# Chunked recurrence of an RWKV block: b and k side by side, u and v on opposite row halves, 128-wide matmuls

## The chip, the cores and the metric

The kernel runs on one core of one Trainium2 chip. The metric is device time in microseconds (us), the median of the runs shown. The engines are TensorE (PE for its matmuls, PEld for its weight loads), VectorE (DVE), ScalarE (ACT), GpSimd (POOL) and SyncE (SP), which issues most DMAs.

## The reference

The program computes a transformer block with attention and a state-space branch, and then a second block. The second block's core is a recurrence that runs in two directions over 256 context tokens and then 1024 tokens, for 8 heads of 64 channels. The change touches this recurrence alone.

```python
def wkv_scan(s0, r, w, k, v, a, b, reverse):
    def step(s, inp):
        r_t, w_t, k_t, v_t, a_t, b_t = inp
        sa = jnp.einsum('bhvk,bhk->bhv', s, a_t)
        s = s * w_t[:, :, None, :] + sa[..., :, None] * b_t[:, :, None, :] + v_t[..., :, None] * k_t[:, :, None, :]
        return s, jnp.einsum('bhvk,bhk->bhv', s, r_t)
    ...
    y, s = lax.scan(step, s0, xs, reverse=reverse)

    # in rwkv_bidir, for each direction d:
    kd = k * (1 + (a - 1) * k_a_h)
    y, s = wkv_scan(s0, r, decay, kd, v, -kk, kk * a, rev)
    y_sum = y_sum + y
```

## The kernel before

`rwkv_chunks` (L2125) does the recurrence in 20 chunks of 64 tokens (`NCK` = 20, `CK` = 64). The first four (`CTX_CK`) are context and give no output; the other 16 do. Both directions d = 0 and 1 run at once, with buffers of their own. A buffer has 128 partitions, two heads of 64 channels one above the other, and `HP` = 4 such pairs behind each other.

For one chunk the steps are these.

- POOL scales the inputs by the decays: `b_raw`, `b_scaled` (L2225, L2232) make b in `bst`; `k_gain`, `k_bias`, `k_raw`, `k_scaled` (L2240 to L2262) make k in `kst`; `a_scaled` and `r_scaled` (L2270, L2280) fill the two halves of `ar`. `v_staged` (L2287) copies v, and `state` (L2295) makes the next state `S` from `sum`. `k_gain` needs the chunk's rates and decays, `ac`, which SP loads two chunks ahead (L2204), once `b_scaled`, `k_scaled` and `r_scaled` of the chunk two before are done.
- PE multiplies b with a and r (`lower`, L2611) and k with a and r (`keys`, L2672). DVE cuts them to triangles with masks in `T.minus` and `T.plus`, into `lm` and `lk` (L2482, L2488), one operation of 512 elements per direction and product.
- A triangular matrix is inverted in levels. Level l is `chained_x` on PE (L2622), `factored` on ACT (L2373), `turned_x`, a transpose, on PE (L2632), `transposed` on ACT (L2378), `advanced` on PE (L2645) and a predicated copy on DVE (L2494). DVE's `first` (L2476) starts it, and `inverted` on PE (L2652) and `inverse` on DVE (L2500) end it.
- With the inverse come the right-hand side, `right_side` and `right_side_of_state` (L2658, L2666), the solution u (`solved`, L2679), the outputs (L2687, L2693) and the next state (L2727). `b_rows`, `k_rows` and `v_rows` (L2698, L2708, L2716) are transposes of b, k and v that `state` and the outputs take.

In `rc_x<-...` and the like, `rc_` is the phase's prefix. Matmuls of 64 rows by 64 columns use one quadrant of the array: `chain`, `crossing` and `staying` (L2575, L2583, L2593) place them. A float32 matmul stands in the trace as two records on PE and two on PEld, a transpose as one on each.

The order of the work is written out by hand. Each engine has one loop over k (POOL L2308, ACT L2406, DVE L2543, PE L2736) in which steps of chunks k - 1, k - 2 and so on are interleaved, and each engine takes its queue strictly in that order. Waits are on semaphores by count. Two of them matter here: POOL's `b_raw` of chunk c waits for the transposes of b of chunk c - 2,

```python
pool.wait_ge(joint["brows_done"], c - 1)
```

and `k_raw` of chunk c for those of k of chunk c - 2 (`rows_done`) and for `keys` (`pk_done`). In POOL's loop `b_raw(k - 1)` stands ahead of the rest of chunk k - 2's scaling:

```python
b_raw(k - 1, 1)
b_raw(k - 1, 0)
k_scaled(k - 2, 1)
...
a_scaled(k - 2, 1)
k_raw(k - 1, 0)
k_gain(k, 0)
k_gain(k, 1)
state(k - 4, 0)
state(k - 4, 1)
```

## Time and profile before

| | |
|---|---|
| runs before | 2673.08, 2678.0, 2678.87 us; median 2678.0 |
| span of the profiled execution | 2672.4 us, 54306 instructions |
| PE busy | 2315.8 us (87%) |
| DVE busy | 1610.5 us (60%) |
| ACT busy | 1047.9 us (39%) |
| POOL busy | 658.7 us (25%) |
| the recurrence's stretch | about 1385 to 1854 us from the span's start |
| DVE `first` of direction 1 starts, chunks 2 and 5 | 1437.65 and 1499.53 us |
| the same, chunks 6 and 18 | 1521.20 and 1798.65 us |

The profiled execution's span of 2672.4 us lies 5.6 us under the median of the runs and 0.7 us under the fastest of them. The shares of busy time are averages over many phases. What bounds the recurrence is read from its own stretch: from the timeline of each engine there, from the waits, and from what ended each of them. "issue" as the releaser of an idle time means that the engine waited for nothing that the profile shows.

### The profile page before, as it was taken

Reading aid. Unit: us, or ns where it says so; the run is one execution under the profiler, and the core shown is the slowest. Engines: PE = TensorE matmul, PEld = TensorE weight load, DVE = VectorE, ACT = ScalarE, POOL = GpSimd, SP = SyncE. Lnnn points to the kernel's source line nnn. Section 1 sums busy time; section 2 is a strip of 40 time slices with the busy share of each in tenths; the row PEclk is TensorE's granted clock in tenths of the full one; section 3 lists DMA queues with packets and bytes.
Section 4 is the critical chain, followed back from the end, with each engine's and each line's share of the span. In section 5 each row is a group of like instructions: output and inputs, shape, how many; then the busy total and the mean of one; then the engine's idle time right before and its main releaser. Section 6 shows DMA issues by size and latency. Waiting matters only on the chain. (4 is left out here: it accounts for less than half of the span.)

```text
span 2672.4 us, 54306 instructions
## 1 busy us (share of the span) xinstructions
PE 2315.8 (87%) x23052; PEld 1827.8 (68%) x23052; DVE 1610.5 (60%) x1961; ACT 1047.9 (39%) x1745; POOL 658.7 (25%) x659
## 2 busy tenths in 40 slices
PE   4998988799989479999758888888983999999993
PEld 2876755468868368888527777776671788888883
DVE  5991659531124555566474444443657999999994
ACT  3112541321022510000345555554231777777773
POOL 0321568113310023222025655551000100000000
PEclk7999999999999689999669999998995999999997
DMA  5232014511122345111161111102232999999994
GB/s 223 99 123 73 1 50 138 157 54 48 52 86 95 108 164 195 63 36 32 44 221 27 28 28 28 28 20 77 96 145 102 376 408 404 397 398 393 396 381 163
DMA packets 135636, 397.84 MB, mean 149 GB/s; under 512 B 56218, under 2 KB 67994, under 8 KB 107890
## 3 DMA queue, kind: packets, MB, share of 16 engines
q1 hardware_dynamic: 124468, 360.02, 36.2%
q0 software_dynamic: 4608, 16.78, 2.6%
q10 hardware_dynamic: 6336, 17.80, 1.8%
q8 instruction: 172, 2.82, 0.4%
q14 instruction: 52, 0.43, 0.1%
HBM read 341.05 MB, written 53.50 MB: 148 GB/s over the span
## 5 line engine op out<-in xcount | busy, mean ns | idle before, releaser
L3871 DVE TENSOR_TENSOR ex_wl<-ew_raw,ex_wh 128x2048 fp32r<-128x2048 f32 x192 | 435.7, 2290 | 41.5 <-ACT ex_wh L3833 38.1
L3833 ACT ACTIVATE ex_wh<-ew_raw 128x2048 fp32r<-128x2048 f32 x192 | 367.7, 1919 | 109.6 <-PE ex_U L3777 40.0
L130 PE MATMUL sp_acc<-b2h_hi,sp_wh 128*128 128x512 f32 (+1 forms) x528 | 195.2, 370 | 14.5 <-POOL sp_wl L1731 14.5
L130 PE MATMUL sp_acc<-b2h_lo,sp_wh 128*128 128x512 f32 (+1 forms) x528 | 195.0, 369 | 0.0
L130 PE MATMUL sp_acc<-b2h_hi,sp_wl 128*128 128x512 f32 (+1 forms) x528 | 194.6, 369 | 0.0
L2494 DVE COPY_PREDICATED rc_x<-b_level,rc_chain 128x256 f32<-128x256 uint32 x160 | 64.5, 445 | 166.2 <-PE rc_chain L2580 165.7
L3754 POOL DMA_INDIRECT x<-ex_o,ex_at x16 | 26.5, 1656 | 494.6 <-DVE ex_o L3894 494.6
L1729 POOL CAST sp_wh<-sp_w 128x1024 fp32r<-128x1024 f32 x26 | 29.1, 1120 | 407.1 <-DMA sp_w<-in_w_conv 230.1
L130 PEld LDWEIGHTS sp_acc<-b2h_hi,sp_wh 128*128 128x128 f32 x528 | 100.3, 190 | 32.3 <-POOL sp_wl L1731 14.9
L2580 PE MATMUL rc_chain<-rc_x,rc_lm 64*64 64x64 f32 x3200 | 94.2, 227 | 20.9 <-issue 14.8
L130 PEld LDWEIGHTS sp_acc<-b2h_hi,sp_wl 128*128 128x128 f32 x528 | 100.3, 190 | 16.5
L130 PEld LDWEIGHTS sp_acc<-b2h_lo,sp_wh 128*128 128x128 f32 x528 | 100.3, 190 | 16.4
L2373 ACT ACTIVATE rc_t<-rc_chain 128x256 f32<-128x256 f32 x200 | 73.7, 387 | 92.6 <-PE rc_chain L2580 90.4
L130 PE MATMUL merge_acc<-merge_hh,merge_wh 128*128 128x512 f32 x256 | 102.9, 402 | 7.7 <-POOL merge_wl L1035 7.2
L130 PE MATMUL pr_acc<-h_hi,pr_wh 128*128 128x512 f32 x224 | 89.5, 399 | 15.9 <-POOL pr_wl L210 14.2
L3775 PE MATMUL ex_G<-ex_wh,ex_xh 128*128 128x512 f32 x256 | 102.0, 398 | 1.4 <-DVE ex_xl L3876 1.4
L130 PE MATMUL merge_acc<-merge_hh,merge_wl 128*128 128x512 f32 x256 | 102.1, 399 | 0.0
L130 PE MATMUL merge_acc<-merge_hl,merge_wh 128*128 128x512 f32 x256 | 101.9, 398 | 0.0
L3775 PE MATMUL ex_O<-ex_wh,ex_hh 128*128 128x512 f32 x256 | 99.8, 390 | 1.6 <-DVE ex_hl L3887 1.6
L3775 PE MATMUL ex_U<-ex_wh,ex_xh 128*128 128x512 f32 x256 | 101.0, 394 | 0.0
L3777 PE MATMUL ex_G<-ex_wh,ex_xl 128*128 128x512 f32 x256 | 100.5, 393 | 0.0
L3776 PE MATMUL ex_G<-ex_wl,ex_xh 128*128 128x512 f32 x256 | 100.1, 391 | 0.0
(522 smaller groups left out, 5983.8 us busy)
## 6 DMA issues: line engine op xcount, KB each, us to landing
ew_raw<-in_exp_gate SPq DMA_DIRECT2D x64, 1024.0 KB, 8.2
ew_raw<-in_exp_up SPq DMA_DIRECT2D x64, 1024.0 KB, 9.3
ew_raw<-in_exp_down SPq DMA_DIRECT2D x64, 1024.0 KB, 7.8
b2p_pT<-in_ada_w SPq DMA_DIRECT2D x32, 512.0 KB, 6.0
rc_ac<-ac SPq DMA_DIRECT2D x40, 256.0 KB, 4.0
b_pj<-in_ada_w SPq DMA_DIRECT2D x8, 1024.0 KB, 12.3
ssm_wm<-in_w_merge SPq DMA_DIRECT2D x16, 512.0 KB, 3.5
ac<-rp_ac SPq DMA_DIRECT2D x4, 2048.0 KB, 7.1
```

Source lines behind the costliest of these rows:

```text
L130: ins = nc.tensor.matmul(out, w[a][:, k, :], h[b][:, k, cols], start=(first and n == 0), stop=(last and n == 2))
L1729: nc.gpsimd.tensor_copy(wh[:, i % 2], w[:]).then_inc(q["w_rounded"], 1)
L2373: A.activation(paired(t[d]["t1"][:]), chained(d), ACT.Copy, scale=-1.0).then_inc(q[d]["t1_ready"], 1)
L2494: V.copy_predicated(paired(b["x"][:, c % 2]), over(T.level[d][l + 1][:].bitcast(u32)), chained(d)).then_inc(s["x_next"], 1)
L2580: last = M(X[d][c * CK:(c + 1) * CK, f, at:at + w], l[k, h], r[k, h], start=True, stop=True)
L3754: nc.gpsimd.indirect_dma_start(x2, bass.IndirectOffsetOnAxis(at[:, x:x + 1], 0), o[:, x % 2, :], None, compute_op=ALU.add).then_inc(scatte ...
L3775: nc.tensor.matmul(acc[:, c], ah[:, k, :], wh[:, s, kk, c], start=(k == 0), stop=False)
L3776: nc.tensor.matmul(acc[:, c], ah[:, k, :], wl[:, s, kk, c], start=False, stop=False)
L3777: last = nc.tensor.matmul(acc[:, c], al[:, k, :], wh[:, s, kk, c], start=False, stop=(k == KD - 1))
L3833: nc.scalar.activation(wh[:, n % RING], raw[:, n % RING], ACT.Copy).then_inc(q["w_hi"], 1)
L3871: V.tensor_tensor(wl[:, n % RING], raw[:, n % RING], wh[:, n % RING].bitcast(f32), ALU.subtract).then_inc(q["w_lo"], 1)
```

## The change

b and k of a head pair now lie side by side in one buffer `bk`, with the two halves swapped between even and odd pairs of heads (`key_slots`). `lower` is one set of matmuls with 128 stationary columns (b and k) and 128 moving ones (a and r), out in `near`; `keys` is gone. The first product, which `first` reads, is made apart by `firsts`, in `crossing`'s bank. `masked` on DVE takes the place of `lower` and `keys` there, two operations of 512 elements per direction. u and v lie in opposite row halves of `uv`, so the outputs and the state are matmuls over all 128 rows (`stacked`) instead of two accumulated ones over 64. The minus signs on u and on the rows of b move into the masks. To fill `uv` ACT evicts u and v by halves of the partitions, four operations each per chunk instead of two. The transposes of b and k come by pairs of heads (`key_rows(c, 0)` where `b_rows` stood, `key_rows(c, 1)` where `k_rows` stood), each with b and k of two pairs, and both `b_raw` and `k_raw` wait for both.

```diff
@@ POOL
                         if c >= 2:
-                            pool.wait_ge(joint["brows_done"], c - 1)
-                        G.tensor_tensor(b["bst"][:, c % 2], nkk[:, :, at(c, d):at(c, d) + CK], b["ac"][:, c % 2, 0], ALU.mult).then_inc(s["b_raw"], 1)
+                            pool.wait_ge(joint["rows_done"], 2 * (c - 1))
+                        G.tensor_tensor(key_slots(d, c)[0], halves(nkk[:, :, at(c, d):at(c, d) + CK]), halves(b["ac"][:, c % 2, 0]), ALU.mult).then_inc(s["b_raw"], 1)
...
                         if c >= 2:
-                            pool.wait_ge(joint["pk_done"], c - 1)
-                            pool.wait_ge(joint["rows_done"], c - 1)
+                            pool.wait_ge(joint["rows_done"], 2 * (c - 1))
@@ ACT
-                    solved(k - 2, 0)
-                    solved(k - 2, 1)
+                    solved(k - 2, 0, 0)
+                    solved(k - 2, 0, 1)
+                    solved(k - 2, 1, 0)
+                    solved(k - 2, 1, 1)
@@ DVE
                     first(k - 1, 1)
-                    lower(k - 1, 1)
-                    lower(k - 1, 0)
                     first(k - 1, 0)
+                    masked(k - 1, 1)
+                    masked(k - 1, 0)
...
-                    keys(k - 1, 1)
-                    keys(k - 1, 0)
@@ PE
+                def stacked(l):
+
+                    for j, e, d, f in product(range(HP // 2), range(2), range(2), range(2)):
+                        at = (2 * d + j) * CK
+                        last = M(W[f * CK:(f + 1) * CK, e, at:at + CK], *l(t[d], f, j, e), start=True, stop=True)
                     return last
...
+                def firsts(c):
+                    if runs(c):
+                        each("b_scaled", c + 1)
+                        each("a_scaled", c + 1)
...
                 def lower(c, d):
                     if runs(c):
                         b, s, sl = t[d], q[d], c % 2
                         pe.wait_ge(s["b_scaled"], c + 1)
+                        pe.wait_ge(s["k_scaled"], c + 1)
...
-                        chain(d, 0, CK, b["ar"][:, sl, :, 0:CK], b["bst"][:, sl])
-                        chain(d, 2 * CK, 2 * CK, b["bst"][:, sl], b["ar"][:, sl]).then_inc(s["low_done"], 1)
+                            pe.wait_ge(s["near_ready"], 2 * c)
+                        for h, f in product(range(HP), range(2)):
+                            k = slice(f * CK, (f + 1) * CK)
+                            last = M(near(d)[:, f, :, h], b["bk"][k, sl, h].rearrange("p a t -> p (a t)"), b["ar"][k, sl, h].rearrange("p (o t) -> p o t", o=2), start=True, stop=True)
+                        last.then_inc(s["low_done"], 1)
...
                 for k in range(NCK + 2):
                     chained_x(k - 2, 0, 4)
                     turned_x(k - 2, 4)
+                    firsts(k - 1)
                     lower(k - 1, 1)
+                    lower(k - 1, 0)
                     right_side(k - 2)
-                    lower(k - 1, 0)
                     inverted(k - 2)
                     chained_x(k - 1, 1, 0)
                     right_side_of_state(k - 2)
                     chained_x(k - 1, 0, 0)
                     turned_x(k - 1, 0)
-                    keys(k - 1)
...
-                    b_rows(k - 1)
+                    key_rows(k - 1, 0)
...
-                    k_rows(k - 1)
+                    key_rows(k - 1, 1)
```

On POOL no row changes its place. In one pass of the loop, from `b_raw` to `a_scaled`, the program before has these rows. A semaphore can stand under the name of one whose number it took over: `n1_inverted` is the one for the transposes of b, `n1_w_loaded7` that of `keys`, `n1_normed` the one for the transposes of k.

```order
L2225 TENSOR_TENSOR rc_bst<-b2k_nkk,rc_ac 128x256 [waits n1_inverted,rc_loaded10]
L2225 TENSOR_TENSOR rc_bst<-b2k_nkk,rc_ac 128x256 [waits n1_inverted,rc_loaded00]
L2262 TENSOR_TENSOR rc_kst<-rc_kst,rc_e_neg 128x256 [waits rc_decays1,rc_k_raw1]
L2280 TENSOR_TENSOR rc_ar<-b2p_pT,rc_e 128x4x64 [waits n1_w_loaded7,rc_decays1]
L2280 TENSOR_TENSOR rc_ar<-b2p_pT,rc_e 128x4x64 [waits n1_w_loaded7,n1_scaled]
L2255 TENSOR_TENSOR rc_kst<-rc_tmp,b2p_pT 128x256 [waits n1_normed,n1_w_loaded7,rc_k_bias1]
L2232 TENSOR_TENSOR rc_bst<-rc_bst,rc_e_neg 128x256 [waits n1_scaled,rc_b_raw0]
L2262 TENSOR_TENSOR rc_kst<-rc_kst,rc_e_neg 128x256 [waits n1_scaled,rc_k_raw0]
L2246 TENSOR_TENSOR rc_tmp<-rc_tmp,rc_ka 128x256 [waits rc_k_gain0]
L2270 TENSOR_TENSOR rc_ar<-b2k_nkk,rc_e 128x4x64 [waits n1_c_ready,rc_decays1]
```

The changed program has the same ten there; `n1_inverted` is now `rows_done`.

```order
L2242 TENSOR_TENSOR rc_bk<-b2k_nkk,rc_ac 128x2x2x64 [waits n1_inverted,rc_loaded10]
L2242 TENSOR_TENSOR rc_bk<-b2k_nkk,rc_ac 128x2x2x64 [waits n1_inverted,rc_loaded00]
L2280 TENSOR_TENSOR rc_bk<-rc_bk,rc_e_neg 128x2x128 [waits rc_decays1,rc_k_raw1]
L2298 TENSOR_TENSOR rc_ar<-b2p_pT,rc_e 128x4x64 [waits rc_low_done1,rc_decays1]
L2298 TENSOR_TENSOR rc_ar<-b2p_pT,rc_e 128x4x64 [waits n1_lo_done,n1_transposed]
L2272 TENSOR_TENSOR rc_bk<-rc_tmp,b2p_pT 128x2x128 [waits n1_inverted,rc_k_bias1]
L2250 TENSOR_TENSOR rc_bk<-rc_bk,rc_e_neg 128x2x2x64 [waits n1_transposed,rc_b_raw0]
L2280 TENSOR_TENSOR rc_bk<-rc_bk,rc_e_neg 128x2x128 [waits n1_transposed,rc_k_raw0]
L2264 TENSOR_TENSOR rc_tmp<-rc_tmp,rc_ka 128x256 [waits rc_k_gain0]
L2288 TENSOR_TENSOR rc_ar<-b2k_nkk,rc_e 128x4x64 [waits n1_c_ready,rc_decays1]
```

Nothing moved in the queue, but the first row and the sixth now wait for one and the same semaphore.

On PE, from the last transposes of chunk k - 2 to the first `advanced` of chunk k - 1, the program before has these rows.

```order
L2604 MATMUL rc_turned<-all_ident,rc_x 128x128 x4
L2580 MATMUL rc_chain<-rc_bst,rc_ar 64x64 x8
L2580 MATMUL rc_chain<-rc_ar,rc_bst 64x128 x8
L2590 MATMUL rc_crossing<-rc_v,rc_lk 64x64 x16
L2580 MATMUL rc_chain<-rc_bst,rc_ar 64x64 x8
L2580 MATMUL rc_chain<-rc_ar,rc_bst 64x128 x8
L2597 MATMUL rc_turned<-rc_xt,rc_t 64x64 x16
L2580 MATMUL rc_chain<-rc_x,rc_lm 64x64 x8
L2597 MATMUL rc_own_half<-rc_S,rc_ar 64x64 x16
L2580 MATMUL rc_chain<-rc_x,rc_lm 64x64 x8
L2604 MATMUL rc_turned<-all_ident,rc_x 128x128 x4
L2590 MATMUL rc_crossing<-rc_ar,rc_kst 64x128 x16
```

The changed program has these.

```order
L2631 MATMUL rc_turned<-all_ident,rc_x 128x128 x4
L2610 MATMUL rc_crossing<-rc_bk,rc_ar 64x64 x16
L2658 MATMUL rc_chain<-rc_ar,rc_bk 128x2x64 x16
L2610 MATMUL rc_crossing<-rc_uv,rc_near 64x64 x16
L2624 MATMUL rc_turned<-rc_xt,rc_t 64x64 x16
L2602 MATMUL rc_chain<-rc_x,rc_near 64x64 x8
L2624 MATMUL rc_own_half<-rc_S,rc_ar 64x64 x16
L2602 MATMUL rc_chain<-rc_x,rc_near 64x64 x8
L2631 MATMUL rc_turned<-all_ident,rc_x 128x128 x4
```

The products of b and k come together ahead of `right_side`, and the 16 matmuls of `keys` between the transposes and `advanced` are gone. Later in the pass the outputs and the state are each one row of 16 matmuls in place of eight rows of 4.

## Rows read from the trace of the kernel before

**Rows 1.** Page, TensorE's granted clock in 40 slices, tenths of full speed.

```profile
PEclk7999999999999689999669999998995999999997
```

**Rows 2.** Windows, three context and twelve output chunks: us, busy (records) by engine.

```profile
1437.65:1499.53 61.88, 54.62 (x1829) 45.88 (x1823) 28.21 (x63) 34.81 (x114) 38.55 (x61) 1.00 0.14 31
1521.20:1798.65 277.45, 236.51 (x8454) 205.07 (x8446) 120.61 (x289) 140.28 (x458) 150.73 (x243) 1.00 0.11 26
```

**Rows 3.** DMA queues, same two stretches (output chunks first): packets, MB, share.

```profile
q8 instruction: 68, 1.11, 1.7%
```

```profile
q8 instruction: 15, 0.25, 1.7%
```

**Rows 4.** Waits of PE: who waited for whom, us in total, times, longest.

```profile
PE rc_chain L2580 <- issue: 28.4, 37, 1.6
```

**Rows 5.** Timeline of PE, an output chunk: start, length, records, [idle before].

```profile
1662.72 1.15 PE L2597 MATMUL rc_own_half<-rc_S,rc_ar 64*64 64x64 f32 x32
...
1665.66 1.10 PE L2590 MATMUL rc_crossing<-rc_ar,rc_kst 64*64 64x128 f32 x32
1666.59 0.64 PE L2580 MATMUL rc_chain<-rc_t,rc_xt 64*64 64x64 f32 x32
...
1674.81 0.66 PE L2604 MATMUL rc_own_half<-all_ident,rc_kst 128*128 128x128 f32 x4
...
1676.91 0.45 PE L2580 MATMUL rc_chain<-rc_x,rc_lm 64*64 64x64 f32 x12 [0.94 <-issue]
...
1682.38 0.46 PE L2580 MATMUL rc_chain<-rc_bst,rc_ar 64*64 64x64 f32 x16
```

**Rows 6.** Timeline of POOL, the same chunk, and two rows of the one before.

```profile
1654.61 0.73 POOL L2262 TENSOR_TENSOR rc_kst<-rc_kst,rc_e_neg 128x256 f32<-128x256 f32 x1
...
1661.44 1.18 POOL L2295 TENSOR_TENSOR rc_S<-rc_sum,rc_e_end 128x256 f32<-128x256 f32 x2
```

```profile
1670.45 1.42 POOL L2225 TENSOR_TENSOR rc_bst<-b2k_nkk,rc_ac 128x256 f32<-128x256 f32 x2 [5.26 <-PE rc_own_half L2604]
...
1672.52 1.32 POOL L2280 TENSOR_TENSOR rc_ar<-b2p_pT,rc_e 128x256 f32<-128x256 f32 x2
1675.63 0.72 POOL L2255 TENSOR_TENSOR rc_kst<-rc_tmp,b2p_pT 128x256 f32<-128x256 f32 x1 [1.79 <-PE rc_own_half L2604]
...
1676.99 0.73 POOL L2262 TENSOR_TENSOR rc_kst<-rc_kst,rc_e_neg 128x256 f32<-128x256 f32 x1
...
1678.25 0.69 POOL L2270 TENSOR_TENSOR rc_ar<-b2k_nkk,rc_e 128x256 f32<-128x256 f32 x1
...
1682.57 0.61 POOL L2240 TENSOR_TENSOR rc_tmp<-rc_ac,rc_ka 128x256 f32<-128x256 f32 x1 [0.24 <-DMA rc_ac<-ac]
1683.14 1.18 POOL L2295 TENSOR_TENSOR rc_S<-rc_sum,rc_e_end 128x256 f32<-128x256 f32 x2
```

**Rows 7.** Timeline of PE, a context chunk: first `advanced`, and `k_rows`.

```profile
1464.02 0.63 PE L2580 MATMUL rc_chain<-rc_t,rc_xt 64*64 64x64 f32 x28
...
1471.15 0.66 PE L2604 MATMUL rc_own_half<-all_ident,rc_kst 128*128 128x128 f32 x4
```

**Rows 8.** Timeline of ACT: the evictions of u in the chunk of rows 5.

```profile
1671.76 0.66 ACT L2388 ACTIVATE rc_u<-rc_crossing 128x256 f32<-128x256 f32 x2 [0.46 <-PE rc_crossing L2590]
```

**Rows 9.** Timeline of PE in an earlier phase, other tile shapes (rows*columns of the array).

```profile
440.45 3.71 PE L896 MATMUL s_pZ<-s_um,s_v 128*64 128x128 f32 x64 [0.48 <-issue]
444.10 3.70 PE L874 MATMUL s_pF<-b_pj 128*128 128x512 f32 x8
```

```profile
458.75 1.16 PE L914 MATMUL s_pB<-s_ca,s_x 64*128 64x128 f32 x16
459.84 0.71 PE L909 MATMUL s_pB<-s_wi,s_um 128*128 128x128 f32 x4
```

**Rows 10.** Windows of PE near chunk 19: us, busy (records), granted clock.

```profile
1819.20:1822.80 3.60, 2.01 (x88) 1.00 0.00 0
1822.80:1826.20 3.40, 3.40 (x84) 0.50 0.02 5
```

201 lines of the change are left out of this document (106 added, 95 removed).

## The prediction, as it stood before the changed kernel ran

> **What bounds the kernel now.** I read the granted clock and the busy shares by slice first [rows 1], then the recurrence alone, for nothing outside it changes. From one start of `first` to the next a chunk with outputs takes 23.1 us (277.45 / 12) and a context chunk 20.6 us (61.88 / 3) [rows 2]. PE is busy 85% of both stretches at full clock; DVE, ACT and POOL are at 43 to 62%.
>
> The next view is what PE's idle time ends on, and most of it is "issue": 28.4 us in 37 waits at one line alone [rows 4]. These gaps stand in the middle of a group of matmuls, as the 0.94 us ahead of the last 12 records of a `chained_x` [rows 5], so no semaphore explains them. The DMA view gives the clue: 68 instruction fetches in the output stretch, one every 4.08 us, and 15 in the context stretch, one every 4.13 us [rows 3]. PE and PEld have 16900 and 3652 records there [rows 2], so 248 and 243 to a fetch, and 16.4 and 16.9 ns to a record. Two stretches with different work thus run at one rate per instruction. I take it that **PE is bound by the fetching of its own code**, at about 16 ns a record, with dependences close behind.
>
> The last view is POOL beside PE, because POOL makes what each chunk starts from. Call S the start of `lower`, A the first `advanced`, K the end of `k_rows`. In the chunk shown K is 1675.47 and the next S 1682.38 [rows 5]. POOL's last operation that `lower` needs ended at 1678.94 [rows 6], 3.4 us early. After S it is `state` that counts: `right_side_of_state` starts at 1662.72, and POOL's states ended at 1662.62 [rows 5, 6]. So that wait is on the edge already, and A follows it.
>
> **The change part by part.** *Fewer PE instructions.* Per chunk `keys` and `lower` have 48 matmuls now and `firsts` and `lower` 32 then; the state goes from 32 to 16, the outputs from 32 to 16. A matmul is four records. That is 192 records less in an output chunk and 128 in a context chunk. At 16.4 ns they would be worth 3.1 and 2.1 us, if fetching stayed the bound. The array's own work hardly falls, because all four quadrants are in use now too: `keys` takes 0.93 us for 16 matmuls of 128 columns [rows 5].
>
> *`b_raw` waits for more.* It waited for the transposes of b, at 1670.45; now it waits for all of `key_rows`, the place of `k_rows`, where `k_raw` waits today, at 1675.63 [rows 6]. Queued behind it on POOL are `k_scaled`, `r_scaled` twice, `k_raw`, `b_scaled`, `k_scaled`, `k_bias` and `a_scaled`, and PE's `firsts` waits for the last. From `b_raw` to the end of `r_scaled` is 3.39 us (1673.84 less 1670.45), from `k_raw` to the end of `a_scaled` 3.31 us (1678.94 less 1675.63), and `k_raw` starts 0.16 us after K. So S comes 0.16 + 3.39 + 3.31 + 0.1 = 6.96 us after K; PE's own work in between fills at most the 6.91 us of this chunk, fetch gap of 0.94 us included. What is late next is `state`. POOL has it behind `k_gain`, which waits for a DMA that is issued once `k_scaled` is done. From the end of `k_scaled` to the end of both states it takes 6.60 us (1684.32 less 1677.72) and in the chunk before 7.28 us (1662.62 less 1655.34) [rows 6]; I take 6.9. Hence K to states is 0.16 + 3.39 + 2.09 (1675.63 to 1677.72) + 6.9 = 12.55 us.
>
> *From there to A.* `right_side_of_state`, `chained_x` and the transposes take some 1.8 us on PE and ACT's copy after them 0.5: an estimate of 2.4 us with a semaphore's delay, where rows 5 show 3.87 us with `keys` (0.93) and one fetch gap (0.7) in it. K to A is then 12.55 + 0.1 + 2.4 = **15.05 us**. The 4.0 us of PE work between S and `right_side_of_state` (`firsts`, both `lower`, `right_side`, `inverted`) and the DVE masks lie beside POOL's states and cost nothing; they end some 1.6 us before the states do.
>
> *From A to K.* In the output chunk it is 8.88 us (1666.59 to 1675.47) [rows 5], about 9.6 in the mean of the period, and in the context chunk 7.79 us [rows 7]. In the output chunk 64 records go, 1.0 us, and waits ahead of A leave fetches time to run ahead: 8.2 us. ACT has two evictions of u more in front of the level-2 `factored`, 0.27 us each by start to start (0.66 less 0.39) [rows 8]; in an output chunk the outputs on PE cover them, in a context chunk they add up to 0.5 us, against 0.4 of fetch gaps gone: 7.9 us. The four evictions of v and the 64-partition shape I price alike; nothing waits on them while POOL is late.
>
> *New shapes.* The outputs become 32 records over 128 rows and 64 columns of the array. 64 such records with 128 moving columns took 3.65 us, 57 ns each, and 16 of the 64-row shape 1.09 us, 68 ns each [rows 9]; half the columns give 0.9 us if the load keeps up and 1.8 us if it doesn't. Now they take 0.95 us. I take 1.1, near the lower end, since the quadrant matmuls keep up already. That makes A to K **8.4 us** with outputs. POOL's strided outputs into `bk` no row shows; below zero is excluded, equal is my value, as `ar` is strided already, and 10% more would be 0.7 us a chunk. The masks are four DVE operations of 512 elements before and after.
>
> The Trainium skill, "TensorEngine Tiling (Array Packing)", Key Properties, says that changing the tiling mode drains TensorE. The trace agrees as far as it goes: in rows 9 the short group costs 0.18 us more than its records at the pace of the long one. The change adds about five such changes of mode to a chunk, two of them between A and K; the rest lie where PE waits. By this rule alone A to K would be 0.35 us longer than the columns give, by the row's 1.1 us it is 0.15.
>
> *The sum.* An output chunk: 15.05 + 8.4 = 23.45 against 23.1 us, +0.35 over 13 chunks: +4.5. A context chunk: 15.05 + 7.9 = 22.95 against 20.6, +2.35 over 3: +7. The first period has no state to wait for: +1.5. The last one with transposes has no `k_gain` ahead of the state: -1.2. After it POOL gates nothing and PE's shorter code counts: -2. Together +9.8 us.
>
> *The clock.* PE will stand idle about 2.5 us ahead of `firsts` and 1.6 us ahead of `right_side_of_state`. After a stretch with 1.6 us idle of 3.6 us the granted clock was 0.50 for the next 3.4 us, the lower of its two levels, 1.2 GHz [rows 10]. Work in such a stretch takes double, so up to 1.7 us late; mostly it falls into the slack ahead of the states. I add 0.3 us for each of 17 chunks: +5. On the span of 2672.4 us this gives 2687, and on the median of 2678.0 about **2693 us**.
>
> **The rivals.** *Fetching stays the bound* and POOL keeps up. Every chunk then gains: 14 x 3.1 + 5 x 2.1 = 54 us, so 2624 us. For it speaks the even rate of records; against it that POOL's queue is strict and its 6.7 us after K stand in the rows. It needs POOL to do the ten operations in under 5 us. Chance 0.05.
>
> *POOL gates, but A to K shrinks to what the dependences ask*, 7.4 us, since the fetches are always ahead. An output chunk is then 22.45 us, -0.65 x 13 = -8.5; with the rest, and no loss by the clock, 2678 - 8.5 + 5.3 = 2675 us. It decides from an A to K under about 7.6 us. Chance 0.17, split between faster and same.
>
> *The new shapes and the clock cost more*: 1.8 us for the outputs (+0.7 x 14 = 10) and a half-speed stretch on the path in each chunk (+1.2 more x 17 = 20): 2723 us. It decides if the low clock lasts beyond `right_side_of_state`. Chance 0.13.
>
> *The change does not take away what it says*: the records per chunk stay. The program's order shows them gone, so I give it nothing.
>
> **How the numbers follow.** My forecast has 0.65, from 2680 to 2708 (A to K and the DMA off by 0.5 us each, over 17 chunks). A measurement of this kernel tells about 0.2% (5.4 us) from no change. Faster by more: the first rival and half of the second, 0.13. Same: the rest of the second and a little of the forecast's low end, 0.15. Slower: 0.72. The range 2669 to 2722 leaves out the first rival, and the ends of the others.
>
> **What would show it.** Right: `b_raw` starts 0.2 us after `key_rows(c, 1)`, `firsts` starts 6.9 to 7.1 us after it on `a_scaled`'s release, K to A is 15 us; context chunks 22 to 23.5 us; fetches 4.6 us apart, few gaps inside groups; dips of the granted clock between 1400 and 1830. Wrong: `firsts` without a wait, context chunks at 18.5 us, or A to K under 7.6 us with outputs.

## The result, and the profile of the changed kernel

The changed kernel took 2720.0 us (median of 4 runs, 2715.6 to 2725.2) against 2676.7 us for the kernel before (4 runs, 2673.1 to 2678.9). The ratio is 1.016, with a 95% interval from 1.014 to 1.017: slower by 43 us. I had forecast 2693 us, slower by 15. The direction and the gate on POOL were right, the size was not. The profiled execution of the changed kernel, 2716.7 us, had a mean granted clock of 0.925 and the other three 0.921 to 0.923, so the profile shows a little less half clock than the median run has.

All but a little of it is in the recurrence. It ended 36.9 us later after the start of the span (1890.2 against 1853.3 us). The span grew by 42.5 us, from 2672.4 to 2714.9. The other 5.6 us lie in the phases behind the recurrence, which the change does not touch. Over the kernels of this study that stretch took from 816 to 828 us in no order that I can relate to the edits, so I give it no cause. Below, K is the end of the last key rows of a chunk (of the k rows in the kernel before), S the start of `firsts` (of `lower` there) and A the first `advanced`; a period goes from one K to the next.

The page of the changed kernel first: TensorE's granted clock in 40 slices, to be laid beside rows 1, and the queue of instruction fetches (packets, MB, share of 16 engines), 159 where the page of before has 172.

```profile
PEclk8999999899999599999769899999995899999996
...
q8 instruction: 159, 2.61, 0.4%
```

The windows view gives the two kinds of chunk: start and end, length, then busy time and records of PE, PEld, DVE, ACT and POOL, granted clock, DMA share, GB/s. The first line is twelve chunks with outputs, from one first `advanced` to another, the second three context chunks, both of the changed kernel. The third is the same twelve output chunks of the kernel before.

```profile
1526.41:1820.06 293.65, 245.72 (x7297) 214.54 (x7297) 122.51 (x290) 162.85 (x505) 149.55 (x240) 0.96 0.11 25
1438.37:1508.40 70.03, 55.58 (x1596) 47.43 (x1596) 26.27 (x59) 40.02 (x125) 37.60 (x60) 0.95 0.11 26
```

```profile
1505.62:1782.75 277.13, 236.32 (x8457) 204.93 (x8452) 122.17 (x290) 140.28 (x457) 150.34 (x240) 1.00 0.12 27
```

An output chunk takes 24.5 us instead of 23.1, though PE executes 193 records less in it (7297 + 7297 over twelve chunks against 8457 + 8452). And the clock is no longer 1.00.

What ends PE's idle time has changed altogether. Where rows 4 had "issue" in the middle of groups, the waits of PE in the twelve output chunks (waiting line, its releaser, us in total, times, longest) now read:

```profile
PE rc_crossing L2610 <- POOL rc_ar L2288: 27.6, 12, 3.4
PE rc_chain L2602 <- ACT rc_xt L2396: 7.5, 13, 0.7
PE rc_crossing L2617 <- ACT rc_uv L2408: 6.3, 11, 0.6
PE rc_chain L2602 <- issue: 4.2, 5, 1.2
```

L2610 is `firsts`: once per chunk it waits 2.3 us for POOL's `a_scaled`. The "issue" gaps have almost gone. The third line is one that I had argued away: the outputs wait for ACT's evictions of u.

The chain from POOL to PE stands in the timelines of one chunk. PE (start, length, tile rows*columns, records, idle time before and its releaser): the outputs and the last key rows, then `firsts`, `lower`, `right_side` and `right_side_of_state`.

```profile
1585.45 1.15 PE L2617 MATMUL rc_crossing<-rc_near,rc_uv 128*64 128x64 f32 x32 [0.59 <-ACT rc_uv L2408]
...
1587.16 0.66 PE L2740 MATMUL rc_own_half<-all_ident,rc_bk 128*128 128x128 f32 x4
...
1594.98 0.69 PE L2610 MATMUL rc_crossing<-rc_bk,rc_ar 64*64 64x64 f32 x32 [2.45 <-POOL rc_ar L2288]
1595.61 2.06 PE L2658 MATMUL rc_chain<-rc_ar,rc_bk 64*128 64x128 f32 x32
1597.60 0.69 PE L2610 MATMUL rc_crossing<-rc_uv,rc_near 64*64 64x64 f32 x32
...
1599.74 1.09 PE L2624 MATMUL rc_own_half<-rc_S,rc_ar 64*64 64x64 f32 x30 [0.30 <-issue]
```

POOL in the same chunk: `b_raw`, `r_scaled`, `a_scaled`, the states.

```profile
1587.96 1.42 POOL L2242 TENSOR_TENSOR rc_bk<-b2k_nkk,rc_ac 128x256 f32<-128x256 f32 x2 [9.97 <-PE rc_own_half L2740]
...
1590.04 1.33 POOL L2298 TENSOR_TENSOR rc_ar<-b2p_pT,rc_e 128x256 f32<-128x256 f32 x2
...
1593.96 0.67 POOL L2288 TENSOR_TENSOR rc_ar<-b2k_nkk,rc_e 128x256 f32<-128x256 f32 x1
...
1598.45 1.18 POOL L2313 TENSOR_TENSOR rc_S<-rc_sum,rc_e_end 128x256 f32<-128x256 f32 x2
```

The key rows end at 1587.82 (1587.16 + 0.66), `b_raw` starts 0.14 us later after 9.97 us of waiting, `a_scaled` ends at 1594.63, and `firsts` starts at 1594.98: K to S is 7.16 us. The states end at 1599.63 and `right_side_of_state` follows 0.11 us behind. That is the chain as forecast.

The new thing is the clock. Here is the same stretch of PE in a chunk five further on:

```profile
1714.10 1.13 PE L2610 MATMUL rc_crossing<-rc_bk,rc_ar 64*64 64x64 f32 x32 [2.44 <-POOL rc_ar L2288]
1715.16 3.78 PE L2658 MATMUL rc_chain<-rc_ar,rc_bk 64*128 64x128 f32 x32
1718.87 1.13 PE L2610 MATMUL rc_crossing<-rc_uv,rc_near 64*64 64x64 f32 x32
...
1721.17 1.04 PE L2624 MATMUL rc_own_half<-rc_S,rc_ar 64*64 64x64 f32 x30
```

And the windows of PE over 6.80 us from `firsts` on, in this chunk and in the undisturbed one (length, busy with records, granted clock):

```profile
1714.10:1720.90 6.80, 6.80 (x134) 0.55 0.36 81
...
1594.90:1601.70 6.80, 6.42 (x196) 1.00 0.35 79
```

The same `lower` takes 3.78 us instead of 2.06. With the clock at 0.50 (1.2 GHz) `right_side_of_state` starts 7.07 us after `firsts` instead of 4.76: the work that was to lie beside POOL's states outlasts them by 2.3 us. Of the 18 periods between key rows, nine contain such a stretch of half clock, 3.4 or 6.8 us long, and in each it sets in within 1.3 us of the start of `firsts`, while PE stands idle there or just after. All five periods in which PE is idle for 3.2 us or more between K and S have one; of the other 13, with 2.1 to 2.5 us, four have. The kernel before has none in its output chunks.

### The profile page after: what moved, and what is told of

Same layout as the page of the kernel before. It is cut to its first block and busy times, and to the rows that moved or that the text cites. A ratio compares the mean times of both kernels' runs of the same rounds, so it can differ in the third digit from the quotient of the medians.

```text
span 2714.9 us, 50905 instructions
## 1 busy us (share of the span) xinstructions
PE 2335.3 (86%) x21292; PEld 1847.0 (68%) x21292; DVE 1611.3 (59%) x1961; ACT 1085.5 (40%) x1825; POOL 660.7 (24%) x659
## 5 line engine op out<-in xcount | busy, mean ns | idle before, releaser
L3803 PE MATMUL ex_O<-ex_wh,ex_hl 128*128 128x512 f32 x256 | 100.7, 393 | 0.0
L3802 PE MATMUL ex_O<-ex_wl,ex_hh 128*128 128x512 f32 x256 | 100.7, 393 | 0.0
```

Source lines behind the costliest of these rows:

```text
L3802: nc.tensor.matmul(acc[:, c], ah[:, k, :], wl[:, s, kk, c], start=False, stop=False)
L3803: last = nc.tensor.matmul(acc[:, c], al[:, k, :], wh[:, s, kk, c], start=False, stop=(k == KD - 1))
```

## Experiments

Times are medians with the ratio to the kernel before in the same rounds; "half clock" is its mean time per output chunk in the profiled execution. Chunk lengths are means of 13 output chunks from K to K. The kernel before took 2671.7 to 2676.7 us in the rounds of the several runs, so a difference of a few us between runs of different rounds says nothing.

| kernel | us | ratio (95%) | output chunk, us | K to S | S to `right_side_of_state` | A to K | half clock |
|---|---|---|---|---|---|---|---|
| before | 2676.7 | 1 | 23.11 | 5.78 | 4.65 | 9.50 | 0 |
| changed | 2720.0 | 1.016 (1.014 to 1.017) | 24.52 | 7.36 | 5.49 | 9.14 | 2.1 |
| e2_late_wait | 2715.6 | 1.015 (1.012 to 1.018) | 25.37 | 7.12 | 5.58 | 9.23 | 2.6 |
| e3_filled_wait | 2706.9 | 1.013 (1.010 to 1.015) | 24.49 | 7.55 | 5.09 | 9.32 | 0.3 |
| e4_split | 2709.5 | 1.013 (1.011 to 1.016) | 24.95 | 5.83 | 5.21 | 10.14 | 0.3 |
| e5_order | 2650.4 | 0.992 (0.989 to 0.994) | 20.92 | 4.80 | 4.37 | 9.08 | 0 |
| e5b_order | 2651.6 | 0.989 (0.987 to 0.991) | 20.87 | 4.81 | 4.34 | 9.09 | 0 |
| e6_before_order | 2671.9 | 0.999 (0.998 to 1.000) | 23.09 | 5.71 | 4.24 | 9.85 | 0.3 |
| e7_order_u | 2641.7 | 0.987 (0.984 to 0.989) | 20.63 | 4.93 | 4.31 | 8.77 | 0 |
| e7b_order_u | 2635.1 | 0.986 (0.984 to 0.988) | 20.57 | 4.93 | 4.29 | 8.70 | 0.3 |
| e8_after_u | 2712.2 | 1.012 (1.010 to 1.014) | 24.55 | 7.37 | 6.12 | 8.56 | 3.9 |
| e9_order_u_split | 2668.0 | 0.999 (0.998 to 1.000) | 22.12 | 4.89 | 6.11 | 8.64 | 0 |
| e10_after_split | 2815.0 | 1.055 (1.051 to 1.058) | 29.94 | 7.37 | 10.41 | 8.94 | 11.6 |
| e11_split_filled | 2727.3 | 1.020 (1.018 to 1.023) | 25.07 | 7.17 | 6.34 | 9.06 | 0.5 |

A 0.3 in the last column is a single stretch of 3.4 us in 13 chunks. In e3, e4, e6 and e7b it sets in 2.6 to 19 us after S, away from the wait ahead of `firsts`. So a rare stretch occurs without that wait too; what the experiments below are about is its coming in half of the periods or more.

### The wait alone (e2_late_wait)

One line of the change, put into the kernel before:

```diff
                         if c >= 2:
-                            pool.wait_ge(joint["brows_done"], c - 1)
+                            pool.wait_ge(joint["rows_done"], c - 1)
```

> The kernel before with one edit: b_raw of chunk c waits for rows_done (c-1), the transposes of the k rows, where it waited for brows_done. Nothing else of the change is in it; PE's 1,792 records per output chunk and the u and v evictions stay. Theory (the gate and what it does to the clock): from the end of k_rows to the start of the next lower 7.1 to 7.2 us instead of 5.8 (7.2 in the profile of the changed kernel), so an output chunk of about 24.4 us instead of 23.1, context chunks about 23 instead of 20.0, which is 13 x 1.3 + 3 x 2.6 = 25 us before the clock; and the longer idle time of PE brings stretches of half clock into the chunks, as in the changed kernel, with 5 to 15 us more. 2,700 to 2,720 us. Rival (PE goes on being limited by the fetches of its own instructions, the wait is taken up by them): under 5 us more than the kernel before, 2,677 to 2,682. Second rival (the half clock comes from the new 128-wide shapes): +20 to +27 us and no half clock between 1,440 us and 1,830 us of the span.

Measured: 2715.6 us. This one wait, with no other part of the change, makes the kernel as slow as the whole change does. The timeline of PE shows the end of the k rows and the next `lower`, 1603.59 to 1610.50:

```profile
1602.93 0.66 PE L2604 MATMUL rc_own_half<-all_ident,rc_kst 128*128 128x128 f32 x4
...
1610.50 0.46 PE L2580 MATMUL rc_chain<-rc_bst,rc_ar 64*64 64x64 f32 x16 [1.27 <-issue]
```

```profile
1517.19:1821.15 303.96, 246.46 (x8457) 215.36 (x8453) 122.03 (x290) 139.72 (x457) 149.83 (x240) 0.95 0.11 25
```

K to S is 6.91 us and the clock 0.95, with the old shapes. So the half clock does not need the 128-wide matmuls, and the fetches of PE's instructions do not hide the wait. Both rivals fall. The chunk is even longer than the changed kernel's (25.4 against 24.5 us; I expected 24.4). The difference lies between `right_side_of_state` and A, 3.45 us against 2.52, where the 16 matmuls of `keys` still stand.

The half clock does not always set in at the same place as in the changed kernel. Of the nine output chunks that have it, three have it from within 1.1 us of S; in the other six it sets in 3.9 to 6.0 us after S, in or within 0.9 us behind a second gap of 1.8 to 2.9 us. That gap is the wait for POOL's states in one case and "issue" in five, where it ends 1.4 to 1.6 us after the end of an instruction fetch. So one later wait brings the half clock, but in this kernel mostly together with a gap of the fetches, and the run does not part the two. The expectation counts 1,792 records in a chunk; the profile has 1409, and 1216 in the changed kernel. The difference of 192 or 193 is the same.

### Work in the wait (e3_filled_wait)

In the changed kernel, five matmuls into a bank that `firsts` overwrites, ahead of its waits:

```diff
                 def firsts(c):
                     if runs(c):
-                        each("b_scaled", c + 1)
-                        each("a_scaled", c + 1)
                         if c >= 2:
                             each("summed", c - 1)
+                            for _ in range(5):
+                                M(W[:, 0, 0:256], T.ident[:], T.masks[0][:].rearrange("p a t -> p (a t)"), start=True, stop=True)
+                        each("b_scaled", c + 1)
+                        each("a_scaled", c + 1)
```

> The changed kernel with five matmuls of 256 columns more per chunk on PE (their result is overwritten and never read), placed where PE waits for POOL's b_scaled and a_scaled ahead of firsts; about 2.1 us of work inside a wait of 3 us or more. Theory (the stretches of half clock follow from PE's idle time at that wait): the stretches inside the output chunks, 2.1 us of half clock per chunk on average, go or become rare, the time from the start of firsts to right_side_of_state falls from 5.5 to 4.7 us, and an output chunk takes 23.6 us instead of 24.5: 13 to 20 us less than the changed kernel, about 2,703. Rival (the half clock follows from what PE does in the rest of the chunk, the 128-column keys gone and 64-row work in their place): the stretches stay, time within 3 us of the changed kernel or above it.

Measured: 2706.9 us, 13 us less than the changed kernel with more work in it. The timeline shows the filler in the place of the idle time, and `lower` at its full speed behind it; the windows view has the clock at 0.99 over twelve output chunks.

```profile
1634.00 2.32 PE L2643 MATMUL rc_crossing<-b_masks,all_ident 128*128 128x256 f32 x10
1636.25 0.72 PE L2610 MATMUL rc_crossing<-rc_bk,rc_ar 64*64 64x64 f32 x32
1636.90 2.06 PE L2660 MATMUL rc_chain<-rc_ar,rc_bk 64*128 64x128 f32 x32
```

```profile
1520.11:1813.99 293.88, 265.37 (x7416) 229.03 (x7417) 121.89 (x290) 162.82 (x505) 149.44 (x240) 0.99 0.11 25
```

Half clock fell from 2.1 to 0.3 us per chunk. The chunk itself did not reach the 23.6 us that I expected: the filler takes 2.3 us and starts only when PE gets to it, so `firsts` came late in half of the chunks (K to S up to 8.2 us). That the stretches follow from what PE does in this wait is shown, and the gain is mostly spent on the filler. Whether the filler helps because it ends the idle time or because it is dense work, this run cannot tell. e5_order below has neither the wait nor a filler, and no half clock in its output chunks.

### More records (e4_split)

In the kernel before, each 128-column matmul of `lower` and `keys` as two of 64 columns:

```diff
-                        last = M(X[d][c * CK:(c + 1) * CK, f, at:at + w], l[k, h], r[k, h], start=True, stop=True)
+                        for o in range(0, w, CK):
+                            last = M(X[d][c * CK:(c + 1) * CK, f, at + o:at + o + CK], l[k, h], r[k, h, o:o + CK], start=True, stop=True)
```

> The kernel before with each matmul of 128 columns in lower and keys issued as two of 64 columns: the same products and columns, 32 matmuls and with them 128 records more per chunk (64 matmuls x 2 records). Nothing of the waits changes. Theory (PE is limited by the fetch of its own records, 16.4 to 16.9 ns each): 128 x 16.4 to 16.9 ns = 2.1 to 2.2 us per chunk, 18 chunks, +35 to +40 us where nothing hides it: about 2,713. Rival (the pauses in the middle of the groups are not the price of a record; the chunk is set by POOL or by the round of dependent steps): the 32 matmuls go into waits, 2,677 to 2,690 us.

Measured: 2709.5 us, 35 us more. The windows view and the instruction queue over twelve output chunks:

```profile
1514.76:1813.40 298.64, 246.55 (x9228) 214.28 (x9224) 121.99 (x290) 140.41 (x456) 150.41 (x240) 0.99 0.11 25
```

```profile
q8 instruction: 74, 1.21, 1.7%
```

A fetch comes every 4.04 us (298.64 / 74), with 9% more records than in the kernel before, where it was 4.08. The chunk grew by 1.84 us, the context chunk by 2.07, against 2.1 forecast from 16.4 ns a record. Not all of it need be fetching: the split groups also take longer on PE itself, `keys` 1.36 us against 1.10 and each 128-column part of `lower` 0.75 against 0.62, some 0.5 us in a chunk.

The traces have a more direct sign. In the twelve output chunks of the kernel before PE has 39 "issue" gaps of more than 0.4 us, 36 us in all, and each of them ends 1.26 to 1.55 us after the end of a fetch in queue q8. Between the gaps PE takes up 32 matmul records and 32 loads in about 0.6 us, about 10 ns each, far faster than the mean of 16.4 ns. So it is the arrival of the code that it waits for, not a fixed pace of issuing.

### POOL's order (e5_order, e5b_order, e6_before_order)

The changed kernel with `b_raw` and `k_raw` behind everything that `firsts` and `lower` need:

```diff
                     a_scaled(k - 2, 0)
-                    b_raw(k - 1, 1)
-                    b_raw(k - 1, 0)
                     k_scaled(k - 2, 1)
                     r_scaled(k - 2, 1)
                     r_scaled(k - 2, 0)
-                    k_raw(k - 1, 1)
                     b_scaled(k - 2, 0)
                     k_scaled(k - 2, 0)
-                    k_bias(k - 1, 0)
                     a_scaled(k - 2, 1)
+                    b_raw(k - 1, 1)
+                    b_raw(k - 1, 0)
+                    k_raw(k - 1, 1)
+                    k_bias(k - 1, 0)
                     k_raw(k - 1, 0)
```

> The changed kernel with POOL's order changed and nothing else: b_raw(k-1) of both directions and k_raw(k-1,1), which wait for key_rows of the chunk before, are put behind a_scaled(k-2,1), so that none of the scaled factors that firsts and lower need stands behind that wait. Theory (the gate makes the time between the key rows and the next firsts, and its idle time makes the half clock): from the end of key_rows to firsts 4.3 to 5.0 us instead of 7.4, PE is limited by its own records again (1,600 per output chunk against 1,792), no half clock, an output chunk of 21.5 to 22.5 us instead of 24.5 and a context chunk of 20 to 21: 30 to 50 us under the changed kernel, 2,670 to 2,690, and 2,640 if the whole of the 192 records is won back. Rival (the new shapes and the two-part evictions are what made the chunk longer): the wait shrinks, but the time from advanced to the key rows grows in its place and the half clock stays; 2,705 to 2,720.

> The kernel of e5_order again, word for word, to stand on the same chip and in the same rounds as e7_order_u: 2,648 to 2,656 us.

> The kernel before with POOL's order of e5_order (b_raw of both directions and k_raw(k-1,1) behind a_scaled(k-2,1)); its own waits and its 1,792 records per output chunk stay. Theory (the kernel before is limited by the fetch of PE's own records, one fetch per 4.07 us, in e4_split too): POOL's order buys it nothing, 2,670 to 2,680 us, fetches 4.1 us apart, pauses inside the groups as before; the 24 us that e5_order is under the kernel before then come from the shorter code. Rival (the order is the gain, the change of shapes brings none of it): 2,650 to 2,660.

Measured: 2650.4 and 2651.6 us, 24 us under the kernel before and 70 and 68 under the changed one; the kernel before with the same order stays where it was (ratio 0.999). I had expected 2670 to 2690 us and a chunk of 21.5 to 22.5; with 20.9 us the gain was larger. On PE the key rows now run into `firsts` without a wait:

```profile
1680.19 0.66 PE L2740 MATMUL rc_own_half<-all_ident,rc_bk 128*128 128x128 f32 x4
...
1685.49 0.69 PE L2610 MATMUL rc_crossing<-rc_bk,rc_ar 64*64 64x64 f32 x32
```

K to S is 4.64 us here, all of it PE's own work, and the clock stays at 1.00. So the gate is not a price of the wide shapes but of POOL's queue: the buffer `bk` comes free late, and what had to wait for that stood ahead of what didn't. The gain needs both halves, the shorter code of the change and the order; either alone gives nothing or a loss.

### The evictions of u (e7_order_u, e7b_order_u, e8_after_u)

The second row half of u goes through DVE, in parallel to ACT:

```diff
 (ACT)
                     solved(k - 2, 0, 0)
-                    solved(k - 2, 0, 1)
                     solved(k - 2, 1, 0)
-                    solved(k - 2, 1, 1)
 (DVE)
                     advanced(k - 1, 0, 1)
+                    solved(k - 2, 0, 1)
+                    solved(k - 2, 1, 1)
                     advanced(k - 1, 1, 2)
```

> e5_order with the second row half of u (rows 64 to 127, both directions) copied out by DVE, which has stood idle 3.5 us at that place, so that ACT and DVE make two operations each side by side. Theory (the four u evictions in a row on ACT hold the outputs back 0.60 us, and in context chunks advanced 1.28 us; but at 20.4 us per chunk PE is already close to its fetch limit): fetches 4.25 us apart there can't come closer than the 4.07 us of the kernel before, 4.9 fetches per chunk, which makes 19.95 us the floor of an output chunk: 0.3 to 0.4 us less per chunk, 5 to 8 us less than e5_order. Rival (no fetch limit near): 0.6 us less per output chunk and 0.5 to 0.8 per context chunk, 10 to 12 us less. Second rival (it was not the u evictions): no change.

> The kernel of e7_order_u again, word for word, in the same rounds as its split form, and to confirm it as the version that is under both kernels: 2,636 to 2,650 us, ratio to the kernel before 0.984 to 0.989.

> The changed kernel with the second row half of u copied out by DVE instead of ACT, nothing else. Theory (the part of the time between advanced and the key rows that was forecast too short, 9.1 us against 8.4, is the wait for the four u evictions, 0.60 us ahead of outputs): 8.5 us between them, an output chunk 0.5 to 0.6 us shorter, 18 chunks, 8 to 11 us less than the changed kernel: 2,706 to 2,712. Rival (the outputs' new shape or the key rows cost it): no change.

Measured: e7_order_u 2641.7 us, 10 us under e5b_order in the same rounds; e7b_order_u, the same kernel, 2635.1 us (just under the 2636 to 2650 expected), 1.4% under the kernel before, the version that beats both. The two engines copy side by side, in the timelines of ACT and DVE at one time:

```profile
1692.99 0.65 ACT L2408 ACTIVATE rc_uv<-rc_crossing 64x256 f32<-64x256 f32 x2 [0.35 <-PE rc_crossing L2617]
```

```profile
1692.99 0.77 DVE L2541 COPY rc_uv<-rc_crossing 64x256 f32<-64x256 f32 x2
```

In the changed kernel one engine had four operations, 1.58 us:

```profile
1583.73 1.58 ACT L2408 ACTIVATE rc_uv<-rc_crossing 64x256 f32<-64x256 f32 x4 [0.62 <-PE rc_crossing L2610]
```

In context chunks A to K fell from 8.49 to 7.23 us. In output chunks the period fell by only 0.24 to 0.30 us in the mean, less than the wait of 0.6 that went. In periods 13 to 15 of e7b_order_u the whole of it shows: 19.65 us against 20.3 in e5b_order. One chunk with a gap of 1.6 us and a stretch of half clock (23.1 us) spoils the mean.

The theory put the small gain down to the fetches. e7b_order_u does have one every 4.11 us (246.38 / 60), near the pace of the kernel before, but the "issue" gaps of PE in the twelve output chunks are only 3.7 us in all, against 38.9 in the kernel before, and PE is busy for 96% of them. So a limit by the fetches is not shown there; it is PE's own work that fills the chunk. The total, 10 us, is what the first rival expected, but from another place: the context chunks gave 1.0 us each, part of which is the half clock that e5b_order had in two of them (against e5_order it is 0.7 us).

```profile
1504.19:1750.57 246.38, 235.43 (x7297) 205.58 (x7297) 131.46 (x314) 150.01 (x481) 150.50 (x240) 0.99 0.13 30
```

```profile
q8 instruction: 60, 0.98, 1.7%
```

e8_after_u has to be read with care. A to K shrank as expected, to 8.56 us with outputs and 7.29 without, yet the output chunk of the profiled execution stayed at 24.55 us: its half clock is 3.9 us per chunk where the changed kernel's was 2.1. Its two output chunks without half clock took 23.6 and 23.1 us, against 23.8 in the changed kernel.

```profile
1525.62:1819.18 293.56, 253.08 (x7296) 222.21 (x7297) 132.57 (x314) 152.43 (x481) 149.84 (x240) 0.92 0.11 25
```

Its median, 2712.2 us, is 8 under the changed kernel's, at the edge of what I expected. The profiled execution was the slowest of its four and had the lowest mean clock of them, 0.918; the other three had 0.922 to 0.925, as the changed kernel's four had 0.921 to 0.925. So the additional half clock belongs to this execution. That shorter work between the waits brings more half clock is not shown.

### A slower `lower` (e9_order_u_split, e10_after_split, e11_split_filled)

Each matmul of `lower` as two of 64 moving columns, in e7_order_u (e9) and in the changed kernel (e10); e11 is e10 with the filler of e3:

```diff
-                            last = M(near(d)[:, f, :, h], b["bk"][k, sl, h].rearrange("p a t -> p (a t)"), b["ar"][k, sl, h].rearrange("p (o t) -> p o t", o=2), start=True, stop=True)
+                            for o in range(2):
+                                last = M(near(d)[:, f, o, h], b["bk"][k, sl, h].rearrange("p a t -> p (a t)"), b["ar"][k, sl, h, o * CK:(o + 1) * CK], start=True, stop=True)
```

> e7_order_u with each 128-column matmul of lower issued as two of 64 columns: the same products, 16 matmuls and 64 records more per chunk, waits unchanged. Theory (e7_order_u is at the limit of PE's instruction fetch again, as the kernel before): 64 x 15.9 to 16.4 ns = 1.0 us per chunk, 18 to 19 chunks: 17 to 20 us more than e7_order_u, 2,659 to 2,663, with fetches 4.0 to 4.1 us apart. Rival (it is limited by the round of dependent steps): 0 to 5 us more.

> The changed kernel with the same split of lower, 64 records more per chunk. Theory (between firsts and right_side_of_state PE's work lies beside POOL's states, and the rate of PE's instructions binds nothing while POOL gates the chunk): the 64 records hide in the 1.6 us of waiting there or take the place of a pause; at full clock no change, and since PE stands idle less, no more half clock than now: 2,712 to 2,724 us, within 4 us of the changed kernel. Rival (records cost their 16 ns everywhere): +1.0 us per chunk, 18 us more, 2,735.

> The kernel of e10_after_split (the changed kernel with lower's matmuls split, 2,815 us, 11.6 us of half clock in an output chunk of 29.9 us) with the five 256-column matmuls of e3_filled_wait put into PE's wait ahead of firsts; their result is overwritten and never read. More work on PE, none removed. Theory (the half clock, here too, begins at the start of firsts because PE stood idle 2.4 us before it, and the slower lower only keeps it low for longer): the half clock goes or is rare, firsts to right_side_of_state takes about 6.1 us as in the one undisturbed chunk of e10_after_split, an output chunk is 24.6 to 25.5 us, and the kernel is some 90 us faster than e10_after_split with more work in it: 2,715 to 2,735 us. Rival (it is the slow 64-row matmuls that hold the clock down, whatever PE did before): the half clock stays at 10 us or more per chunk, 2,800 us or above.

Both expectations for e9 and both for e10 missed. In e9 the group takes 3.84 us instead of 2.06:

```profile
1701.47 3.84 PE L2666 MATMUL rc_chain<-rc_ar,rc_bk 64*128 64x64 f32 x64
```

```profile
1510.57:1775.65 265.08, 254.66 (x7680) 225.97 (x7681) 133.01 (x314) 150.31 (x481) 150.74 (x241) 1.00 0.12 28
```

That is 60 ns a record against 64 for the 128-column form: half the moving columns, nearly the same time. So it is not the moving side that sets the time of this shape, and the row of the weight loads points to the stationary one. It has 64 loads behind each other, 58 ns from one to the next, through nearly the whole group:

```profile
1701.46 3.70 PEld L2666 LDWEIGHTS rc_chain<-rc_ar,rc_bk 64*128 64x128 f32 x64
```

With 1.78 us more in the group, and 1.55 more in an output chunk, e9 is 33 us slower than e7b_order_u (2668.0 against 2635.1), nearly twice what the fetches would have asked; they come every 4.28 us now and do not bind. The Trainium skill, "TensorE: Matmul & The Clock Gate", section "LDWEIGHTS (loading the stationary operand)", says that a load's time goes with its columns and not with its rows. The trace agrees in kind: loads of 128 columns come 58 ns apart here, whatever moves, and those of 64 columns in `firsts` about 18 ns apart (0.56 us for 32). (Four quadrants are in use in `firsts` and two row halves here, so the two figures differ by more than the columns.) By the formula of that section of the Trainium skill a load of 128 columns is about 107 ns; as an estimate the 32 loads of the unsplit group would be 3.4 us one after another and 1.7 two at a time, in the two row halves. They take 1.86 us, and no run here tells the two apart.

In e10 the same 1.8 us were to vanish beside POOL's states. Instead the kernel lost 95 us:

```profile
1711.99 1.13 PE L2610 MATMUL rc_crossing<-rc_bk,rc_ar 64*64 64x64 f32 x32 [2.45 <-POOL rc_ar L2288]
1713.05 7.14 PE L2659 MATMUL rc_chain<-rc_ar,rc_bk 64*128 64x64 f32 x64
```

```profile
1712.00:1742.70 30.70, 27.10 (x642) 0.78 0.09 20
```

The half clock sets in within 2.4 us of the start of `firsts` in all but one case, as in the changed kernel, but it lasts longer, 13.7 us in each of the last nine periods. In the one chunk that escaped, `right_side_of_state` came 6.07 us after S and the chunk took 24.6 us; the last nine take 30.6 to 31.3. My claim that less idle time means less half clock was wrong here.

e11 decides between the two readings. It has the same slow `lower` and more work still, only the wait is filled:

```profile
1645.82 2.32 PE L2643 MATMUL rc_crossing<-b_masks,all_ident 128*128 128x256 f32 x10
1648.08 0.69 PE L2610 MATMUL rc_crossing<-rc_bk,rc_ar 64*64 64x64 f32 x32
1648.70 3.84 PE L2661 MATMUL rc_chain<-rc_ar,rc_bk 64*128 64x64 f32 x64
```

```profile
1528.45:1829.21 300.76, 283.68 (x7801) 0.99 0.11 25
```

2727.3 us, 88 less than e10. And e9, with the same slow `lower` and no wait ahead of it, ran at 1.00. So the drop comes from the wait, and with the slow group behind it, it lasts longer. Whether the filler acts by ending the idle time or by being dense work stays open for e11, as for e3; e9 has no filler. Why it lasts 13.7 us there and 3.4 or 6.8 in the changed kernel, these runs don't settle.

## Why the prediction was right or wrong

The path was right: `b_raw` waits for the key rows, POOL gates `firsts` and the states, and the clock falls at that wait. The steps that failed are terms of the sum. The largest is the clock: 0.3 us for each of 17 chunks, 5 us, on the ground that the doubled work falls into the slack ahead of the states, where the stretches cost 11. The other is A to K, priced at 8.4 us where it took 9.2. DVE's work beside POOL, 3.4 us, was put at nothing. The sections below take the terms one by one; of the 28 us that the forecast missed, 22 are in the recurrence and 5.6 behind it.

**What bounds the kernel now: right.** PE was limited by its instruction fetches. e4_split charged 35 us for 128 records a chunk and no columns, where 16.4 ns a record made 38, and every longer "issue" gap of the kernel before ends behind a fetch. (PE was busy 85% of the output stretch, as the prediction says, but 88% of the context stretch.)

**The gate: right.** `b_raw` 0.14 us after the key rows (0.16 forecast), K to S 7.16 us (6.96), states to `right_side_of_state` 0.11 us (0.1). e2_late_wait shows that this wait makes the slowdown by itself. In undisturbed output chunks K to A is 14.6 us against 15.05, since the states end 6.2 us after `k_scaled` (1593.42 to 1599.63), sooner than the 6.9 us that I took.

**A to K: mis-sized, 8.4 us against 9.2 in undisturbed output chunks.** The failed step is "in an output chunk the outputs on PE cover them", of the two evictions of u more. The outputs read u. They don't cover its evictions, they wait for them: 0.59 us in the timeline, 6.3 us in the twelve chunks. The price of an eviction was too low as well: the four start 0.40 us apart (1.58 us in all), where the two of the kernel before started 0.27 apart (0.66 us), so the two more cost 0.9 us and not 0.54. In context chunks A to K is 8.5 us against 7.9. e8_after_u took the wait away and gave 8.56 us, and 7.29 in context chunks. In the undisturbed chunk the errors of K to A and A to K partly cancel, which is luck: 23.80 us (mean of seven) against 23.45.

**The new shapes: right where it was measured.** The outputs take 1.15 us, 1.1 forecast. The rival's 1.8 us is refuted. What a change of tile shape costs by itself no run separates. The 0.18 us that I read out of rows 9 for it is mostly something else: at 64 ns a record, the pace of the same 64*128 shape in `lower`, the 16 records make 1.03 of the 1.09 us, so those rows do not show a price of the change.

**The clock: the place was right, the size was not.** I had the place (idle ahead of `firsts`) and added 0.3 us for each of 17 chunks, 5 us, on the grounds that doubled work "mostly falls into the slack ahead of the states". A stretch costs 0.6 to 1.9 us where it occurs, for the slack was smaller than I had it. PE's work from S to `right_side_of_state` takes 4.3 us where nothing delays it (e5_order), and the states come 4.65 us after S in the undisturbed chunk, not 5.6: some 0.4 us of slack where I had 1.6. Against undisturbed chunks of the same kind the nine periods lost about 11 us. The rival that had a stretch of it in every chunk, for 20 us more, overshot: half of the periods escaped.

**Left out: DVE's other work in four chunks.** In the fourth to the seventh period DVE has one operation of other work (`weigh`), and the two `b_raw` beside it take 2.17 to 2.41 us instead of 1.42 (K to S 7.9 to 8.1 us instead of 7.15):

```profile
1536.07 2.40 POOL L2242 TENSOR_TENSOR rc_bk<-b2k_nkk,rc_ac 128x256 f32<-128x256 f32 x2 [10.19 <-PE rc_own_half L2740]
```

```profile
1536.50 1.38 DVE L3540 TENSOR_TENSOR b2p_ow<-b2p_ow,b2p_gate_row 128x1024 f32<-128x1024 f32 x1
```

In the kernel before `weigh` fell elsewhere: the five `b_raw` pairs of that stretch took 1.42 us each. Now it lies on the gated path and costs 3.4 us in all. The rows that I used came from chunk 12.

**The ends.** The first period cost 3.3 us beside its half clock instead of 1.5. The last one with transposes was to gain 1.2 us and, half clock aside, lost 0.4. The tail gained 0.7 us, not 2, and the first key rows came 1.3 us later. I had measured context chunks from `first` to `first`, which gave 20.6 us as their length, where K to K gives 20.0: 1.7 us.

The working of the difference in the recurrence, 36.9 against 14.8 us forecast: output chunks 13 x 0.35 = 4.6, context chunks 0.2 and their base 1.7, half clock 11 - 5 = 6, DVE's work 3.4, first period 1.8, last 1.6, the two ends 2.6. Together 21.9 of 22.1 us. The 5.6 us behind the recurrence come on top and are not explained by the change.

**The rivals.** That fetching stays the bound needed POOL's ten operations in under 5 us after K; e5_order shows what it takes, not faster operations but another order of them, and it then gave 2650 us rather than the 2624 that I had for it. There the round of dependent steps, with the waits for u and for ACT's copies at the first `advanced`, sets in before the whole of the 190 records is won back: 2.2 us of 3.1 per chunk. In e5b_order those two waits come to 1.2 us a chunk (14.1 us in twelve).

## What to carry to other kernels

When two buffers are joined into one, list for every writer which reader now frees it, and then look at what stands behind that writer in its engine's queue: moving three writers behind work that didn't need the buffer turned +43 us into -24. When a wait grows on TensorE, price the work behind it at half clock as well as at full, and count the slack against the doubled time. A wait of 2.4 us can cost more in the clock than in itself (4.9 us a chunk between e10_after_split and e11_split_filled), and the cheap test is to fill it with dummy matmuls and see whether the kernel gets faster. Before reading a change of the clock out of one profile, compare the mean clock of all executions.

## What the runs showed of the hardware

- One wait of POOL made later, which makes PE wait longer in every chunk, changed the clock of twelve output chunks from 1.00 to 0.95 with no other edit (e2_late_wait); 1.8 us more of slow matmuls behind such a wait cost 5.4 us per chunk, and 2.3 us of dummy matmuls in the wait took 88 us off the kernel (e10_after_split, e11_split_filled).
- PE can be held back by the arrival of its own instructions. In the kernel before and in e4_split, with 1409 and 1538 records of PE and PEld per output chunk by the windows view, a fetch comes every 4.08 and 4.04 us, and the "issue" gaps of more than 0.4 us end 1.26 to 1.55 us after the end of a fetch in the kernel before (39 of 39) and between 1.2 and 1.6 us in e4_split (47 of 50). No kernel here fetches faster. Where something else binds, the fetches come every 4.11 us (e7b_order_u), 4.16 (e5b_order), 4.28 (e9_order_u_split) or 4.98 (the changed kernel).
- A matmul of 64 rows and 128 stationary columns takes 60 to 64 ns a record whether 64 or 128 columns move through it (e9_order_u_split, the changed kernel). Splitting its moving side nearly doubles the time of the group (2.06 to 3.84 us). Splitting the 64*64 matmuls of `keys` in the kernel before took their group from 1.10 to 1.36 us (e4_split).
- The two `b_raw` of POOL, 1.42 us, take 2.17 to 2.41 us with one operation of DVE of 1.2 to 1.4 us beside them (four chunks of the changed kernel).
- The amount of half clock differs between executions of one kernel: the mean clock of e8_after_u was 0.918 in one and 0.922 to 0.925 in three others.
